# Fourteen seven-product pairs behind four plain tiles, instead of thirteen behind six, in the MLPs of a two-block transformer kernel

## What is computed

```python
def sq_relu_mlp(h, w1, w2):
    a = jax.nn.relu(h @ w1)
    return (a * a) @ w2

h = h + sq_relu_mlp(rms_norm(h, norm_mlp_g[l]), mlp_w1[l], mlp_w2[l])
```

## Time and profile before

| | |
|---|---|
| median of three runs | 2167.26 us (2166.2 to 2167.39) |
| the profiled execution, its own time | 2166.9 us |
| its span, first to last instruction | 2164.7 us |
| PE busy, of the span | 99% |
| DVE busy | 69% |
| ACT busy | 46% |
| granted TensorE clock, mean | 0.999 of full speed |
| pair 1 of the first MLP | 1235.60 to 1256.02 us |
| first matmul of the MLP, first and second layer | 1201.55 and 1820.17 us |

### The profile page before, as it was taken

The page is one execution under the profiler, slowest core; times in us unless marked ns, Lnnn a source line. Parts: engine busy times, 40 slices in busy tenths (PEclk is TensorE's granted clock), DMA queues, the critical chain, the costliest instruction groups (busy, mean ns, idle before and its releaser), DMA issues.

```text
span 2164.7 us, 35259 instructions
## 1 busy us (share of the span) xinstructions
PE 2150.4 (99%) x13776; PEld 1907.5 (88%) x13776; DVE 1494.7 (69%) x2518; ACT 999.1 (46%) x1724; POOL 14.5 (1%) x14
## 2 busy tenths in 40 slices
PE   9999999999999999999999999999999999999998
PEld 7887888888778888898898899999888888999998
DVE  5866665558666567586766777776887658777775
ACT  5445533434546345375554544444534435544444
POOL 0000000000000000200000000000000000000000
PEclk9999999999999999999999999999999999999999
DMA  5655443336645333454344232323223212233231
GB/s 205 180 180 160 154 128 104 114 117 186 189 139 156 126 97 112 140 178 157 115 151 138 97 106 98 113 103 100 96 88 117 88 49 98 99 107 104 100 115 55
DMA packets 136709, 268.37 MB, mean 124 GB/s; under 512 B 21773, under 2 KB 79931, under 8 KB 136160
## 3 DMA queue, kind: packets, MB, share of 16 engines
q1 hardware_dynamic: 136544, 266.13, 38.1%
HBM read 235.37 MB, written 26.77 MB: 121 GB/s over the span
## 4 chain that ended last, share of the span: by engine, by line
PE 97%; DVE 1%; ACT 1%; issue 0%; DMA 0%; SPq 0%; DVEq 0%; ACTq 0%
PE ps L2366 30%; PE ps L2367 30%; PE ps L2372 30%; PE ps L2387 2%; PE ps L2398 2%; PE ps L2422 0%; PE ps L2424 0%; PE ps L2412 0%; PE ps L2411 0%; PE ps L2423 0%; PE ps L2410 0%; PE ps L2441 0%; DVE t_X L3084 0%; DVE t_SQ L2742 0%; DMA t_X<-in_xT 0%
## 5 line engine op out<-in xcount | busy, mean ns | idle before, releaser
L2366 PE MATMUL ps<-t_P0H,t_whi 128*128 128x512 f32 (+1 forms) x1072 | 418.3, 390 | 1.9 <-DVE t_P0L L2734 1.9
L2367 PE MATMUL ps<-t_P0L,t_whi 128*128 128x512 f32 (+1 forms) x1072 | 412.4, 385 | 0.0
L2372 PE MATMUL ps<-t_P0H,t_wlo 128*128 128x512 f32 (+1 forms) x1044 | 402.8, 386 | 0.0
L2689 DVE TENSOR_TENSOR t_wlo<-t_raw,t_whi 128x1024 fp32r<-128x1024 f32 (+1 forms) x262 | 309.2, 1182 | 40.5 <-PE ps L2372 29.2
L2513 ACT ACTIVATE t_whi<-t_raw 128x1024 fp32r<-128x1024 f32 (+1 forms) x267 | 270.8, 1021 | 82.3 <-PE ps L2372 80.1
L2366 PEld LDWEIGHTS ps<-t_P0H,t_whi 128*128 128x128 f32 x1072 | 201.3, 188 | 54.5 <-issue 14.4
L2367 PEld LDWEIGHTS ps<-t_P0L,t_whi 128*128 128x128 f32 x1072 | 201.5, 188 | 38.9 <-issue 1.0
L2372 PEld LDWEIGHTS ps<-t_P0H,t_wlo 128*128 128x128 f32 x1044 | 196.1, 188 | 40.1
L2366 PE MATMUL ps<-t_PRH,t_MH 128*128 128x256 f32 x832 | 229.6, 276 | 0.0
L2367 PE MATMUL ps<-t_PRL,t_MH 128*128 128x256 f32 x832 | 229.6, 276 | 0.0
L2372 PE MATMUL ps<-t_PRH,t_ML 128*128 128x256 f32 x832 | 229.6, 276 | 0.0
(11 more groups left out here) (385 smaller groups left out, 4868.0 us busy)
## 6 DMA issues: line engine op xcount, KB each, us to landing
t_raw<-in_wts SPq DMA_DIRECT2D x362, 512.0 KB, 3.5
far<-t_Tb SPq DMA_DIRECT2D x26, 384.0 KB, 3.1
far<-t_Tb SPq DMA_DIRECT2D x16, 512.0 KB, 3.8
t_PTX<-far SPq DMA_DIRECT2D x64, 96.0 KB, 3.4
t_raw<-in_wts SPq DMA_DIRECT2D x16, 384.0 KB, 3.2
t_QKV<-far SPq DMA_DIRECT2D x32, 128.0 KB, 2.7
t_raw<-in_wts SPq DMA_DIRECT2D x13, 256.0 KB, 2.8
t_PTX<-far SPq DMA_DIRECT2D x24, 128.0 KB, 3.0
```

Source lines behind the costliest of these rows:

```text
L2366: e.matmul(s.out, s.sh, s.mh, start=s.first, stop=False, skip_group_check=again)
L2367: e.matmul(s.out, s.sh, s.ml, start=False, stop="halved" in s, skip_group_check=again)
L2372: i = e.matmul(s.out, s.sl, s.mh, start=False, stop=s.end, skip_group_check=again)
L2689: e.tensor_tensor(s.dst, s.raw, s.hi.bitcast(F32), ALU.subtract).then_inc(*mark("lo", s.j))
```

## The change

The MLP starts with four plain tiles instead of six, and the two hidden tiles that are no longer plain become pair 0, ahead of the thirteen pairs that there were. The strips of w1 and their order stay.

Around pair 0, only two tiles of the second product stand, not four: `other(0)` and `other(3)` do nothing there, and `other(1)` and `other(2)` run the first two tiles of chunk 0. Every later pair takes the four tiles that follow those, so that a pair now ends one chunk's half in its middle; behind the last pair two tiles of chunk 6 are left instead of four. The preparation of the first pair keeps its distance to the pair (its u0 two plain tiles ahead, its sums one), and so falls two plain tiles earlier in the stage, among the last `combine` steps. The number of tiles and weight blocks, and the bytes loaded, are the same; the raw slots are dealt out in another rotation. The second MLP is changed in the same way.

```diff
-        w0 = [Weight(chunk("mlp_w1", l, halves(0), halves(128 * i, 1))) for i in range(6)]
+        w0 = [Weight(chunk("mlp_w1", l, halves(0), halves(128 * i, 1))) for i in range(4)]
         raws = {}
-        for n in range(1, 14):
-            cols, c, m = 512 + 256 * n, (n - 1) // 2, 4 * ((n - 1) % 2)
+        beside = [(0,)] + [(2 * n - 1, 2 * n) for n in range(1, 14)]
+        for n in range(14):
+            cols = 512 + 256 * n
             raws[n] = [own(chunk("mlp_w1", l, halves(0), halves(cols + 128 * i, 1))) for i in range(2)]
-            raws[n] += [own(chunk("mlp_w2", l, halves(512 * c, 4), halves(128 * m + 256 * i, 2))) for i in range(2)]
+            raws[n] += [own(chunk("mlp_w2", l, halves(512 * (i // 4), 4), halves(256 * (i % 4), 2))) for i in beside[n]]
...
         combine("high 3")
+        u0(0)
+        w2(0, 0)
         run(first_tile(2, w0[2]))
         combine("low 3")
+        low(0, "u0")
+        low(0, "w0", 2)
+        sums(0)
+        u1(0)
+        u2(0)
         run(first_tile(3, w0[3]))
-        u0(1)
-        w2(1, 0)
-        run(first_tile(4, w0[4]))
-        low(1, "u0")
-        low(1, "w0", 2)
-        sums(1)
-        u1(1)
-        u2(1)
-        run(first_tile(5, w0[5]))
-        low(1, "u1", 0)
-        low(1, "u2", 1)
-        u3(1)
+        low(0, "u1", 0)
+        low(0, "u2", 1)
+        u3(0)
...
             def other(i):
 
-                run(second_tile(c2, m2 + i, u[f"w{i // 2}"], i % 2, two=True))
+                if n == 0:
+                    if i in (0, 3):
+                        return "mm", tiles[0] - 1
+                    flush()
+                    i -= 1
+                at = beside[n][i // 2]
+                run(second_tile(at // 4, 2 * (at % 4) + i % 2, u[f"w{i // 2}"], i % 2, two=True))
                 return "mm", tiles[0] - 1
...
-            if n == 1:
+            if n == 0:
                 low(n, "u3")
-                w2(n, 1)
             else:
                 low(n, "w1", 3)
...
             other(0)
-            if n == 1:
-                low(n, "w1", 3)
...
-        for n in range(1, 14):
+        for n in range(14):
...
-        run(second(6, 4))
+        run(second(6, 6))
```

More of the change, by code:

```diff
@@ L1808, in sums @@
                 s = emit("sums", t=S1, a11=raw_of(i, 0, 512), a12=raw_of(i, 512, 512), a21=raw_of(j, 0, 512),
-                         a22=raw_of(j, 512, 512), need=[landed(j), U[n]["u0"].key] + (tfree if n == 1 else []))
+                         a22=raw_of(j, 512, 512), need=[landed(j), U[n]["u0"].key] + (tfree if n == 0 else []))
                 U[n]["sums"] = s.id
@@ L1858, in pair_of_tiles @@
             more = n + 1 < 14
-            c2, m2 = (n - 1) // 2, 4 * ((n - 1) % 2)
             def other(i):
-                run(second_tile(c2, m2 + i, u[f"w{i // 2}"], i % 2, two=True))
+                if n == 0:
[5 more added lines that the diff above has]
+                run(second_tile(at // 4, 2 * (at % 4) + i % 2, u[f"w{i // 2}"], i % 2, two=True))
                 return "mm", tiles[0] - 1
```

## The result

| | before | the change |
|---|---|---|
| median of 11 executions, side by side | 2167.39 us | 2173.96 us |
| lowest and highest | 2166.20 and 2169.26 us | 2173.15 and 2186.08 us |
| ratio, 95% interval | | 1.0043, 1.0030 to 1.0056 |
| the profiled execution, and its span | 2166.9, 2164.7 us | 2185.05, 2183.2 us |

The ratio is that of the means, 2176.89 to 2167.46. The forecast was 2173.2 us, with 2169.5 to 2176.5 as its range. The median lies inside and the mean just above it, but the executions do not lie around either. They form groups: eight at 2173.15 to 2174.45, three at 2184.79 to 2186.08, and nothing between. With the seven more of the change that the experiments bring, there are 10 at 2173.15 to 2176.05, 7 at 2184.5 to 2186.08 and one at 2196.3.

The account below looks back on a forecast made before the run. PE, busy 99% of the span, was taken to bound the kernel. Per layer, 4.66 us of waits and restart less 1.67 saved gave 2.99, 6.0 in all: 2166.9 + 6.0 = 2172.9, plus 0.36 for the median, 2173.2 us; range 2169.5 to 2176.5.

Parts of the forecast that it names:

- What PE saves: Per layer, 48 matmuls of 512 columns go (11.20 us) and 84 of 256 come (9.53): 1.67 us less.
- What feeds pair 0: DVE's and ACT's rows ahead of pair 0: its sums come 10.00 us earlier, the pair itself 11.20.
- First wait: In pair 0, PE waits ahead of T2 for ACT's copy s1, until 1229.92: 2.78 us.
- Second wait: Inside pair 0's `other(1)`, PE waits for DVE's low part of the fourth plain relu: 1.7 us.
- Sum: Per layer 4.51 us lost to waits, 0.15 for a restart, 1.67 saved: 2.99 more, 6.0 in all.
- Edits that I cost at nothing: Later pairs' cover, chunks changing mid-pair, two tiles behind the last pair, loads: no cost; T2 of pair 1 might wait some tenths.
- nothing new later: Sign of a right forecast: after pair 0's two gaps in each layer, no new PE gap.
- The clock falls in the gaps: Rival: pair 0's gaps take the clock to 1.2 GHz, 3 us per layer taken, 2179 us; 10%.
- What a matmul takes is read from windows that begin and end at a stage's first matmuls: Plain-tile and pair 1 windows before the change: 0.2333 us per 512-column matmul, 0.1134 per 256-column one.
- my rivals: Cover holds, 2163.9 us, 6%; one wait only, 2169.8, 11%; clock falls in pair 0's gaps, 2179, 10%.

Follow-up runs that it names:

- the first experiment: The changed kernel run again with no edit: 2174.21, 2176.05 and four executions at 2184.5 to 2185.03 us.
- the covered version: The change with pair 0's preparation, the copy s1 and the fourth relu's low part all moved earlier: 2164.12 us, ratio 0.9985 to the kernel before.
- the kernel with gaps: The kernel before, with the first second-product tile moved behind T2 in pairs 2, 4, ... 12, so PE waits there: 2201.83 us.
- one gap of 1.46: The change with the copy s1 and the fourth relu's low part both moved earlier in pair 0: ten executions at 2167.01 to 2169.01 us, two at 2178.73 and 2178.8.
- gaps of 0.24 and 1.58: The change with only pair 0's preparation moved ahead: 2168.98 and 2170.0 us, three at 2179.8 to 2180.98, one at 2190.61.

## Why the prediction was right and wrong

- *What PE saves*, 1.67 per layer: right. With all waits covered the gain is 2167.46 - 2164.12 = 3.34, twice that (1.3 to 5.2 by the interval).
- *What feeds pair 0* and *First wait*: right. 2.63 to 2.64 us in all six layers profiled, where I had 2.78.
- *Second wait*: right in its mechanism and size, 1.7 said, 1.71 and 1.72 us measured in the two layers in which the clock stayed up. In the others PE came later, and the wait is 0.3 or nothing.
- *Sum*: 2173.2 said; the middle of the lowest group is 2173.8. The median of the first eleven lies near it because eight of them had no wide layer; of the six executions of the first experiment only two had none, and their median is 2184.6.
- *Edits that I cost at nothing*: nearly right. PE has no gap in pairs 1 to 13, and the median gain of the covered version leaves little room for a cost in the chunks that change in the middle of a pair. One start is late by 0.2 us in the second layer (a distance of 0.31 at 2152.41), among the half-width tiles of chunk 7; I had said "nothing new later".
- *The clock falls in the gaps*: the mechanism came true, in four of six layers, and I gave it 10%. Its price was wrong. I let the slow stretch reach beyond the end of the second wait and put 3 us per layer on it; mostly some 16 matmuls ran slow (1.6 us), and the wait for DVE took that in. The case that I thought would be dear is mostly free, and cost up to 1.8 only where the second wait was gone.
- **The step that failed** is the first one: "What a matmul takes is read from windows that begin and end at a stage's first matmuls". I read 0.1134 from a pair of the kernel before and carried it to all pairs behind the gaps. Shape and clock do not fix this distance. Behind a gap it can come back wide and stay so to the end of the MLP, 11 us per layer, and by the groups it did in a quarter of the change's layers; the pairs of the kernel before have no gap among them. My range ended at 2176.5, below 8 of 18 executions, and none of my rivals had them. Rows of the profile before could have warned me; these three stretches of it, all without a gap and at a clock of 1.00, hold 256-column matmuls, two of the attention ahead of the MLP and one of the MLP's pairs:

```profile
1111.00:1117.00 6.00, 6.00 (x54) 6.00 (x53) 2.65 (x5) 3.08 (x7) 0.00 (x0) 1.00 0.27 90
1134.00:1140.00 6.00, 6.00 (x56) 6.00 (x55) 5.30 (x10) 4.34 (x7) 0.00 (x0) 1.00 0.88 272
1280.00:1300.00 20.00, 20.00 (x179) 20.00 (x179) 14.98 (x21) 8.74 (x14) 0.00 (x0) 1.00 0.32 107
```

The first goes by 0.118 us, the wide spacing, the second by 0.113, the narrow one, as the MLP's pairs do. I had read only the pairs. The attention also shows that the spacing can turn without a gap: between 1100.6 and 1157.9 it turns eight times, though no two neighbouring starts lie more than 0.13 us apart. In nine of the ten profiles it does so at the same eight places, to one matmul (the tenth has a short gap there). So in the attention it goes with the place in the program, while behind a gap in the MLP it differed from one execution to the next. What turns it is shown in neither.

## What to carry to other kernels

In a dense stretch of matmuls a gap may cost more than its length. It can take the clock down, and it can leave the spacing wider, for as long as the stretch lasts: here 11 us per layer behind gaps of 2.6 us and, by the times, behind gaps of 1.5. So a saving that opens a gap in the longest dense stretch is worth taking only with the gap closed, by moving the feeders' rows. When executions of a kernel fall into groups, count matmuls per stretch in profiles of several executions before looking for a wait; one profile, and one median, would have hidden it.

## What the runs showed of the hardware

- Two spacings of the same matmuls (128 x 256, float32 operands in two parts) at the same granted clock of 1.00, 0.1133 and 0.1178 us, each steady over hundreds of us in the MLP. A restart can change it either way: from narrow to wide behind a gap of 1.44 us in pair 8 of the kernel with gaps, back behind one of 1.34 in pair 12. In the attention it turns without one. What decides, and whether the share truly differs between gaps (by the groups 9 of 36 layers in the change, 2 of 24 with one gap of 1.46, 5 of 12 with gaps of 0.24 and 1.58), is open. The Trainium skill, "TensorE: Matmul & The Clock Gate", section "Back-to-back issue gap", says that in a stream the distance is set by the weight load and the matmul together, and gives 0.1092 us for the isolated matmul, an estimate by its formula. Both measured spacings are wider, and no run here shows which part the loads have in them.
- The granted clock stayed at 1.00 behind every gap of 1.34 to 1.72 us in the MLPs (14 restarts in these profiles), fell to half behind three of six of 2.29 to 2.39, and behind seven of ten of 2.63 to 2.75. The same gap in the same place fell in one execution and not in the next. Once down, it stayed so for 14 to 17 matmuls in most cases and for 28 in two. The Trainium skill, same page, section "HAM oscillation", warns of idle gaps between dense matmuls, and the runs agree that such a gap can take the clock down. What they add is that the same gap does not always do so; what decides is not shown, so a forecast has to carry it as a chance.
